# Four lanes of the neighbourhood attention, each one step behind the one before it

## The reference

```
s_win = einsum('bwhd,brwchd->bhwrc', qr, k_win) * scale + bias
s_ctx = einsum('bwhd,blhd->bhwl', qr, kc) * scale
p = softmax(concatenate([s_win, s_ctx], -1))
o = einsum('bhwrc,brwchd->bwhd', p_win, v_win) + einsum('bhwl,blhd->bwhd', p_ctx, vc)
```

## Time and profile before

| what | value |
|---|---|
| timed runs, median of 3 | 3470.05 us (3467.31 to 3479.96) |
| profiled execution, device time | 3491.03 us |
| its span, first to last instruction | 3489.2 us |
| busy in the span: TensorE, VectorE, ScalarE, GpSimd | 92%, 49%, 33%, 4% |
| mean granted clock of TensorE | 0.928 |
| the stage that changes | 3101.0 to 3238.4 us |

### The profile page before, as it was taken

One profiled execution on the slowest core, in us unless ns is written; L12 is line 12 of the kernel. 1 busy time (PEld: TensorE's weight loads), 2 busy tenths in 40 slices (PEclk: granted clock), 3 DMA queues, 4 the chain that ended last, 5 costly groups with the idle time before them and its releaser, 6 DMA issues.

```text
span 3489.2 us, 38836 instructions
## 1 busy us (share of the span) xinstructions
PE 3196.8 (92%) x15576; PEld 2546.7 (73%) x15576; DVE 1710.5 (49%) x2771; ACT 1152.8 (33%) x1855; POOL 141.4 (4%) x145
## 2 busy tenths in 40 slices
PE   7999798888888989999999997779999979987998
PEld 6888476677767778888788885458888456877886
DVE  5434543555565554344743447755344445336235
ACT  3323233433343343233332233543222233323332
POOL 0000000121111100000000000000000000000000
PEclk9999999788897899999999998689999979997998
DMA  3333231000000033323233322002323410201231
GB/s 125 97 98 97 66 103 34 3 3 3 3 5 13 1 121 97 103 91 103 79 97 97 97 85 76 1 31 91 102 93 101 155 51 1 76 19 46 79 95 57
DMA packets 173896, 234.76 MB, mean 67 GB/s; under 512 B 14201, under 2 KB 111062, under 8 KB 173462
## 3 DMA queue, kind: packets, MB, share of 16 engines
q1 hardware_dynamic: 173718, 232.29, 21.3%
HBM read 228.05 MB, written 4.19 MB: 67 GB/s over the span
## 4 chain that ended last, share of the span: by engine, by line
PE 83%; DVE 10%; ACT 4%; issue 2%; POOL 1%; DMA 1%; SPq 0%; ACTq 0%; DVEq 0%
PE banks L795 61%; PE banks L894 3%; PE banks L1216 3%; PE banks L1210 1%; PE banks L888 1%; PE banks L1204 1%; PE banks L956 1%; PE banks L929 1%; PE banks L1156 1%; PE banks L952 1%; PE banks L903 1%; DVE diff_scores L2176 1%; DVE diff_small L2182 1%; PE banks L859 1%; DVE kv_tmp L1836 1%
## 5 line engine op out<-in xcount | busy, mean ns | idle before, releaser
L1749 DVE TENSOR_TENSOR weights_lo<-weights_raw,weights_hi 128x1024 fp32r<-128x1024 f32 (+2 forms) x393 | 473.3, 1206 | 1061.1 <-ACT weights_hi L1284 1059.8
L795 PE MATMUL banks<-operand_hi,weights_hi 128*128 128x512 f32 x2208 | 873.5, 396 | 32.5 <-DVE weights_lo L1749 19.0
L795 PE MATMUL banks<-operand_lo,weights_hi 128*128 128x512 f32 x2208 | 866.7, 393 | 0.0
L795 PE MATMUL banks<-operand_hi,weights_lo 128*128 128x512 f32 x2208 | 866.2, 392 | 0.0
L1284 ACT ACTIVATE weights_hi<-weights_raw 128x1024 fp32r<-128x1024 f32 (+2 forms) x393 | 408.4, 1041 | 1116.7 <-PE banks L795 1058.6
L795 PEld LDWEIGHTS banks<-operand_hi,weights_hi 128*128 128x128 f32 x2208 | 418.8, 190 | 127.0 <-issue 25.4
L795 PEld LDWEIGHTS banks<-operand_lo,weights_hi 128*128 128x128 f32 x2208 | 419.1, 190 | 89.0 <-issue 2.4
L795 PEld LDWEIGHTS banks<-operand_hi,weights_lo 128*128 128x128 f32 x2208 | 418.8, 190 | 88.6
L894 PE MATMUL banks<-operand_lo 128*128 128x512 f32 x424 | 214.3, 533 | 1.3 <-ACT v L1394 1.3
L795 PE MATMUL banks<-hidden_ffn_hi,weights_hi 128*128 128x512 f32 x352 | 136.9, 389 | 0.0
L795 PE MATMUL banks<-hidden_ffn_lo,weights_hi 128*128 128x512 f32 x352 | 136.9, 389 | 0.0
(11 more groups left out here) (500 smaller groups left out, 4526.0 us busy)
## 6 DMA issues: line engine op xcount, KB each, us to landing
weights_raw<-in_ffn_w_in_dram SPq DMA_DIRECT2D x352, 256.0 KB, 3.0
weights_raw<-in_ffn_w_out_dram SPq DMA_DIRECT2D x88, 512.0 KB, 3.7
weights_raw<-in_w_in_dram SPq DMA_DIRECT2D x36, 512.0 KB, 3.6
weights_raw<-in_rwkv_w_rkv_dram SPq DMA_DIRECT2D x24, 512.0 KB, 3.8
weights_raw<-in_w_mod_dram SPq DMA_DIRECT2D x24, 512.0 KB, 4.8
weights_raw<-in_w_kv_dram SPq DMA_DIRECT2D x16, 512.0 KB, 3.6
weights_raw<-in_rwkv_w_o_dram SPq DMA_DIRECT2D x8, 512.0 KB, 5.6
weights_raw<-in_diff_w_q_dram SPq DMA_DIRECT2D x8, 512.0 KB, 4.4
```

The source lines that it names most:

```text
L795: mm = nc.tensor.matmul(o, l, r, start=first and t == 0 and job["opens"], stop=last and t == 2, **skip)
L1749: nc.vector.tensor_tensor(ring_lo[0:p, u["slot"], 0:n, 0:w], ring_raw[0:p, u["ring"], 0:n, 0:w], f32(ring_hi[0:p, u["slot"], 0:n, 0:w]), A ...
```

## The change

The table becomes two. The latent attention keeps the one without stagger; the neighbourhood attention gets one made with stagger on. Both are still walked by all engines and by the table of expected semaphore values. Nothing else is changed.

```diff
--- before.py
+++ after.py
@@ -505,10 +505,10 @@
         operand_plan("cq", 2)
         add_dense("uq", "act", n=4)
         close("uq")
-        ATTN_ORDER = woven(MLA_HEADS, 5 * TB, LANES, False)
+        ATTN_ORDER = {"mla": woven(MLA_HEADS, 5 * TB, LANES, False), "na": woven(NA_HEADS, 5 * TB, LANES, True)}
 
         def attention_plan(name):
-            for hd, lane, s in ATTN_ORDER:
+            for hd, lane, s in ATTN_ORDER[name]:
                 tb, s = divmod(s, 5)
                 if s == 0:
                     lane_pe[lane].expect((name, "s", hd, tb))
@@ -526,7 +526,6 @@
                     lane_pe[lane].expect((name, "o", hd, tb))
                     lane_dve[lane].expect((name, "o", hd, tb))
 
-        attn_lane = {hd: lane for hd, lane, s in ATTN_ORDER}
         attention_plan("mla")
         close("mla")
 
```

## The result

| | median, us | lowest to highest | runs |
|---|---|---|---|
| before | 3475.0 | 3467.3 to 3489.0 | 4 |
| changed | 3568.2 | 3546.6 to 3570.5 | 4 |

The ratio is 1.0235, with a 95% interval of 1.0204 to 1.0266: the kernel became slower by 71 to 92 us. In the profiled executions the span went from 3489.2 to 3568.7 us, +79.5.

The account below looks back on a forecast made before the run. TensorE was taken as the bound: 32 lane turns of 6.93 us at 1.2 GHz make the stage 84 us longer, +85 in all, put onto the 3470.05 us median for 3555 us. Range 3465 to 3575, the forecast's own 3545 to 3572.

Parts of the forecast that it names:

- The idle stretch: TensorE's 3.3 us wait between scores and transposes in each of 8 neighbourhood-attention rounds goes: -26 us.
- The clock: Neighbourhood attention starts at 1.2 GHz and its new mixture never earns full clock back: 27.7 us a round, not 14.8.
- the two stretches of the earlier trace: In the differential attention, TensorE busy 13.40 of 13.40 and 13.50 of 13.50 us, yet at clock 0.50.
- the first wait: At the stage's start TensorE idles 3.2 us before the first transposes, which sets the low clock.
- the comparison with the differential attention: Its similar alternation stayed at 0.50 for over 13 us; the new mixture is thinner, with lone scores and 64-column values.
- The page's rule on the clock: Skill page: low clock is the default, sustained activity releases it; the prediction held that the earlier trace disagrees for 13 us.
- rival 1: The clock is soon full in the neighbourhood attention: -16 us, 3453 us, or 3460 if recovery takes 14 us; chance 0.17.
- The prices: TensorE's cost per lane at 1.2 GHz: scores 3.1, values 2.55, transposes 1.28, sum 6.93 us; at full clock 3.7.
- the change of array: Switching between half and whole array around lone scores: 0.4 us each at full clock, 0.4 to 0.6 at low clock.
- The sum: Stage ends at 3322.6 against 3238.36, +84 us; in all +85, a median of 3555 us.
- the dense stage behind: The stage after neighbourhood attention starts at the low clock: +1 us.
- The size of the low clock in the old order: In each neighbourhood-attention round before, 24 transposes took 5.4 us instead of 2.8: 2.6 us for the low clock.

Follow-up runs that it names:

- fill_start: Changed kernel plus seven idle products in TensorE's first wait of the neighbourhood-attention stage; 0.9926 of the kernel before, median 3460.9 us, stage 120.4 us.
- fill_less: Changed kernel plus three idle products in the stage's first wait; runs of 3561.6, 3455.6, 3563.5 and 3546.5 us, no ratio given.
- burst_middle: Changed kernel plus fourteen idle products in one run halfway through the stage, none at its start; 1.0070 of the kernel before, stage 172.3 us.
- full_rows: Changed kernel with every head's scores taken over all 128 rows, so not the reference's scores; 0.9905 of the kernel before, stage 113.6 us.
- wide_values: Changed kernel with each value product taking 128 columns, half of the result used; 0.9969 of the kernel before, stage 126.3 us.
- before_filled: Kernel before, old order, plus seven idle products in TensorE's wait of each of the 8 rounds; 0.9969 of the kernel before, stage 127.4 us.
- pairs: Against the changed kernel, lanes 0 and 1 run in step, 2 and 3 two steps behind; 0.9930 of the kernel before, 0.9922 with seven idle products at the start.

## Why the prediction was right

**The idle stretch goes: right.** TensorE's waits of 3.3 us per round are gone, and VectorE never held it up.

**The clock: right, and it was the step that mattered.** 0.50 from 3105.7 to the end of the stage, as forecast from the two stretches of the earlier trace rows and the first wait. fill_start, fill_less and burst_middle show that what goes before picks the speed. full_rows and wide_values show what keeps the low one: the mixture has two thin parts, scores on 64 rows and values of 64 columns, and lifting either of them brought the clock back, after 3.4 and 10.1 us. The prediction gave both reasons, and drew the comparison with the differential attention from them. That the amount of arithmetic is what counts is the simplest account of the two, and is argued, not shown; for the scores, the rows in use and the changes of array were lifted together.

**The page's rule on the clock.** The Trainium skill, "TensorE: Matmul & The Clock Gate", Part 1, has sustained activity release the low clock. By that rule, as the prediction took it, rival 1 would have come true; here a TensorE that was busy 213.66 of 214 us was not released. The measurement decides: having an instruction in flight all the time was not enough here.

**The prices.** A lane at 1.2 GHz was put at 6.93 us and took 6.89. That this is so near is in part luck: scores were put at 3.1 and took 2.85, values were put at 2.55 and took 2.75 in the chain, above the upper bound of 2.6, and the two misses cancel. In the scores the change of array cost 0.27 us at the low clock, 2.85 against 2.58 for scores on 128 rows in full_rows, and 0.19 at the full one, 1.48 against 1.29, so it grew by less than the factor of two between the clocks. At full clock 3.70 was forecast and 3.63 measured in fill_start, 120.3 us for the stage against 121. The first transposes were put at 3105.75 and came at 3105.38.

**The sum.** The stage was forecast 84 us longer and is 81.8; the profiled span rose by 79.5, where I had 85. The 1 us more for the dense stage behind was not seen: from the last output to the end it took 1.8 us less than before. The timed median of 3568.2 lies 13 us above the forecast 3555. 5 of it are the median of before, which rose from the 3470 that I started from to 3475; the other 8 are that the medians differ by 93 us and the forecast by 85. Of the four timed runs one took 3546.6, some 20 us less than the others. The four runs of the kernel before spread as widely, from 3467.3 to 3489.0. That run has no profile, and what made it shorter stays open.

**The size of the low clock in the old order** was over-read: I gave each round 2.6 us for it. before_filled shows 1.4. It didn't enter the forecast, where the low clock decides all, but it would have been wrong as a gain.

## What to carry to other kernels

A TensorE that is busy without a pause can still run at half speed for a whole stage: read the granted clock beside the busy time, and ask of a new order which run of work in it can win the clock back after the first wait. Here a few idle products in the one wait ahead of the stage (99 us), or value products widened into columns that cost next to nothing (93 us), were worth far more than the waits that the stagger removed, which went from 27.0 to 3.3 us. Two products that use two halves of the array are best moved together: the pairs had the shortest stage of all.

## What the hardware showed that was not expected

- One program gives 3455.6 and 3563.5 us on the same chip (fill_less). Its start has a pause of 1.8 us, some 460 us before its end, behind which the clock fell in the profiled run.
- Products that compute nothing, or twice the columns needed, made the changed kernel faster: the stage takes 126.3 us with 128-column values and 219.1 with 64-column ones.
- Whether the clock comes back depends on what TensorE does, not on its being busy: after 3.4 us with 128-row scores, 3.3 us with twelve transposes and the first values, 10.1 us with half-array scores and wide values, 12.7 us with staggered 96-row scores, and not in 214 us with lone 64-row scores and 64-column values. These are single profiles; one unchanged sequence took 3.8 to 7.0 us, so the short ones are not to be ranked.
